# The front of a two-block kernel: modulation chunks in turns of shift and scale, tokens pair by pair, x by tiles

## The reference, cut to what matters

```python
mod = silu(cond) @ w_mod + b_mod            # for x and for ctx: shift, scale, gate of 1024 each, and more for the next layer
y = x * rsqrt(mean(x * x, -1) + 1e-6) * norm_pre
h = y * (1 + scale) + shift                 # the tokens; the same for ctx with its own modulation
px, pc = h_x @ w_in_even, h_ctx @ w_in_even # then rope, differential attention, short convolution, gates, ...
lam = ...exp of two dot products of lam_a   # used in the attention, together with subln
```

## Time and profile before

| | us |
|---|---|
| median of 3 runs | 1631.51 (1627.53 to 1632.32) |
| span of the profiled execution | 1629.8 |
| TensorE matmuls busy | 1520.9 (93%) |
| TensorE weight loads | 1289.6 (79%) |
| VectorE / ScalarE / GpSimd busy | 743.1 / 670.7 / 407.3 |

### The profile page before, as it was taken

How to read it: one execution, slowest core, us unless ns; L and a number is a source line. 1 busy time by engine, 2 the same in 40 slices (tenths; PEclk the granted TensorE clock), 3 DMA queues, 4 the chain that set the end, 5 groups by cost and what they waited for, 6 DMA issues and landing times. The chain is left out here.

```text
span 1629.8 us, 29981 instructions
## 1 busy us (share of the span) xinstructions
PE 1520.9 (93%) x12637; PEld 1289.6 (79%) x12637; DVE 743.1 (46%) x1258; ACT 670.7 (41%) x1098; POOL 407.3 (25%) x106
## 2 busy tenths in 40 slices
PE   4999998889989999998999999978879999999998
PEld 4888897777778888987879897847868888888786
DVE  5344247678645511137854424468654333433002
ACT  5301326666653311137754544372354344344212
POOL 1322221211030243230012432200043343444342
PEclk9999999999999999999999999999999999999999
DMA  9344463335040032046220431000021323222321
GB/s 375 114 156 156 157 180 73 83 80 130 1 174 33 3 130 96 31 147 162 47 104 28 153 123 68 1 0 4 4 105 52 109 98 103 103 82 73 129 90 65
DMA packets 32600, 155.78 MB, mean 96 GB/s; under 512 B 6745, under 2 KB 8281, under 8 KB 18017
## 3 DMA queue, kind: packets, MB, share of 16 engines
q1 hardware_dynamic: 31456, 153.83, 28.4%
q10 hardware_dynamic: 1024, 0.21, 0.1%
HBM read 132.01 MB, written 2.10 MB: 82 GB/s over the span
## 5 line engine op out<-in xcount | busy, mean ns | idle before, releaser
L215 PE MATMUL banks<-ffn_token_parts,ffu_weight_parts 128*128 128x512 f32 (+1 forms) x1056 | 229.6, 380 | 1.2 <-POOL ffu_weight_parts L196 0.9
L215 PEld LDWEIGHTS banks<-ffn_token_parts,ffu_weight_parts 128*128 128x128 f32 x1056 | 191.7, 188 | 38.9 <-POOL ffu_weight_parts L196 1.1
L196 POOL TENSOR_TENSOR even_weight_parts<-weight_chunk,even_weight_parts 128x2048 fp32r<-128x2048 f32 x15 | 70.2, 4683 | 308.7 <-ACT even_weight_parts L190 308.7
L196 POOL TENSOR_TENSOR ffu_weight_parts<-weight_chunk,ffu_weight_parts 128x2048 fp32r<-128x2048 f32 x22 | 101.6, 4619 | 157.3 <-ACT ffu_weight_parts L190 157.3
L215 PE MATMUL banks<-even_token_parts,even_weight_parts 128*128 128x512 f32 (+1 forms) x672 | 124.8, 345 | 0.0
L993 PE MATMUL banks<-even_token_parts,even_weight_parts 128*128 128x512 f32 (+1 forms) x576 | 122.4, 348 | 0.0
L3235 PE MATMUL banks<-ffd_weight_parts,ffn_f_parts 128*128 128x512 f32 x528 | 120.1, 389 | 1.7 <-PEq L3136 1.7
L215 PEld LDWEIGHTS banks<-even_token_parts,even_weight_parts 128*128 128x128 f32 x672 | 103.6, 188 | 19.4 <-issue 3.8
L3235 PEld LDWEIGHTS banks<-ffd_weight_parts,ffn_f_parts 128*128 128x128 f32 x528 | 99.0, 188 | 22.6 <-issue 2.1
L215 PE MATMUL banks<-sec_token_parts,sec_weight_parts 128*128 128x512 f32 (+1 forms) x528 | 115.0, 375 | 0.3 <-PEq L285 0.3
L3213 DVE SCALAR_TENSOR_TENSOR ffn_conv<-banks,b_ffn_taps,ffn_conv 128x511 f32<-128x511 f32 (+1 forms) x88 | 61.8, 744 | 110.7 <-ACT ffn_conv L3185 107.6
(11 more groups left out here) (468 smaller groups left out, 2796.9 us busy)
## 6 DMA issues: line engine op xcount, KB each, us to landing
weight_chunk<-in_ffn_up SPq DMA_DIRECT2D x22, 1024.0 KB, 4.8
weight_chunk<-in_w_in_even SPq DMA_DIRECT2D x16, 1024.0 KB, 7.1
front_late<-in_w_mod SPq DMA_DIRECT2D x16, 1024.0 KB, 5.0
weight_chunk<-in_w_in SPq DMA_DIRECT2D x13, 1024.0 KB, 5.0
weight_chunk<-in_w_out SPq DMA_DIRECT2D x12, 1024.0 KB, 5.4
weight_chunk<-in_w_in_odd SPq DMA_DIRECT2D x12, 1024.0 KB, 4.8
weight_chunk<-in_ffn_down SPq DMA_DIRECT2D x11, 1024.0 KB, 4.9
front_w<-in_w_mod SPq DMA_DIRECT2D x8, 1024.0 KB, 23.5
```

What stands on the lines that cost most here:

```text
L196: (on or self.nc.gpsimd).tensor_tensor(parts[:, 1], self.env.raw[s][:], parts[:, 0].bitcast(F32), ALU.subtract).then_inc(self.lo_done, 1)
L215: m = self.nc.tensor.matmul(o, w, env.tok[:, tp, k, a:b], start=n == 0, stop=n == 3 * KD - 1)
```

## The change

The eight chunks of the front are taken in turns of shift and scale, so that a pair (one shift, one gain chunk) covers two k tiles. The slots in memory are reordered to match. TensorE interleaves: products of pair q with the chunks of pair q + 1, whose columns follow the low products. The transposes run x first (all eight k), then ctx, and both evacuating engines share both kinds. x is loaded as four tiles, each with its semaphore, and x and ctx have a root each. The value tile is cleared by GpSimd and not by VectorE. Five of the seven small loads move from ScalarE's queue to SP's, behind the bulk; the lambda work, which needs them, moves behind the early tiles. The silu of cond is done before the bias loads are issued.

```diff
+MOD_ORDER = 0, 4, 1, 5, 2, 6, 3, 7
...
-        slot_homes = [env.tok_at + s * slot_bytes for s in range(4)] + [env.parts_at + (2 + s) * slot_bytes for s in range(2)]
-        slot_homes += [homes["head_hi"], homes["pT"] + 8 * NT * D]
+        slot_homes = [env.tok_at + s * slot_bytes for s in (0, 3, 1, 4, 2, 5)] + [homes["head_hi"], homes["pT"] + 8 * NT * D]
...
-        SMALL = 16 * 7
+        SMALL, LATER = 16 * 2, 16 * 5
...
+        turns = [*range(0, 2 * KD, 2), *range(1, 2 * KD, 2)]
...
-                sp.dma_start(env.X[:], A["x"].rearrange("(t p) d -> p t d", p=P)).then_inc(x_in, 16)
+                for t in range(TX):
+                    sp.dma_start(env.X[:, t, :], A["x"][t * P : (t + 1) * P]).then_inc(x_in[t], 16)
                 sp.dma_start(env.CX[:], A["ctx"].rearrange("(t p) d -> p t d", p=P)).then_inc(c_in, 16)
-                for n in range(MOD_FIRST):
-                    if n == 3:
+                for a, n in enumerate(MOD_ORDER):
+                    if a == 1:
                         weights(0)
-                    sp.dma_start(slots[n][:], A["w_mod"][n]).then_inc(w_in[n], 16)
+                    sp.dma_start(slots[a][:], A["w_mod"][n]).then_inc(w_in[a], 16)
                 weights(1)
                 sp.dma_start(tables[:], A["rope"]).then_inc(tables_in, 16)
                 sp.dma_start(exchange[:], A["rope_swap"]).then_inc(tables_in, 16)
-                sp.wait_ge(scaled, TX)
+                sp.dma_start(taps[:], A["conv_b"]).then_inc(later_in, 16)
+                sp.dma_start(env.pre2[:], A["pre_mix"]).then_inc(later_in, 16)
+                sp.dma_start(env.pre_ffn[:], A["pre_ffn"]).then_inc(later_in, 16)
+                sp.dma_start(lam[:], A["lam_a"].partition_broadcast(P)).then_inc(later_in, 16)
+                sp.dma_start(env.subln[:], A["subln"]).then_inc(later_in, 16)
+                sp.wait_ge(scaled, 2)
+                sp.wait_ge(scaled_late, 2)
...
+                nc.gpsimd.memset(v_flat, 0.0).then_inc(cleared, 1)
...
                 pe.wait_ge(cond_ready, 1)
-                pe.wait_ge(small_in, SMALL)
                 mod(0)
+                for i in range(KD // 2):
+                    turn_in(i)
                 mod(1)
                 columns(0)
-                mod(2)
+                for i in range(KD // 2, KD):
+                    turn_in(i)
                 columns(1)
...
+                for i in range(KD, 2 * KD):
+                    turn_in(i)
                 pe.wait_ge(raw_even, KD)
                 pe.wait_ge(raw_odd, KD)
...
+                for q in range(KD // 2):
+                    following = range(2 * q + 2, min(2 * q + 4, MOD_FIRST))
+                    for i, k in enumerate((2 * q, 2 * q + 1)):
+                        token_hi(k)
+                        for n in following[i : i + 1]:
+                            mod(n)
+                    if q < KD // 2 - 1:
+                        for i, k in enumerate((2 * q, 2 * q + 1)):
+                            for f in range(2):
+                                token_lo(k, f)
+                            for n in following[i : i + 1]:
+                                columns(n)
+                    else:
+                        for f in range(2):
+                            for k in (2 * q, 2 * q + 1):
+                                token_lo(k, f)
                 late_mod(0)
                 exchanged(0)
...
+                act.wait_ge(cond_in, 16)
+                nc.scalar.activation(cond[:], cond[:], ACT.Silu).then_inc(cond_ready, 1)
                 act.wait_ge(cleared, 1)
                 for j in range(4):
                     act.dma_start(bmod[32 * j : 32 * j + 2], A["b_mod"][j]).then_inc(bias_in, 16)
...
+                act.wait_ge(mean_c, 1)
+                nc.scalar.activation(ss[:, TX:NT], ss[:, TX:NT], ACT.Sqrt).then_inc(root_c, 1)
+                raw(0)
+                act.wait_ge(inverse_c, 1)
...
+                for i in range(2, KD, 2):
+                    raw(i)
                 ring.hi(act, 0, 0)
...
+                for i in range(KD, 2 * KD, 2):
+                    raw(i)
                 act.wait_ge(raw_odd, KD)
                 for q in range(KD // 2):
-                    act.wait_ge(affine, MOD_FIRST // 2 + 1 + q)
+                    act.wait_ge(affine, 2 * q + 2)
                     for j in range(4 * q, 4 * q + 4):
                         affined(j, job_part(j, 0)).then_inc(hi_done, 1)
                     affined(4 * q + 3, job_norm(4 * q + 3)).then_inc(normed_c_odd, 1)
...
                 for q in range(KD // 2):
-                    dve.wait_ge(affine, MOD_FIRST // 2 + 1 + q)
+                    following = range(2 * q + 2, min(2 * q + 4, MOD_FIRST))
+                    dve.wait_ge(affine, 2 * q + 2)
                     normed(4 * q, normed_x)
                     normed(4 * q + 1, normed_c_even)
                     normed(4 * q + 2, normed_x)
-                    if q < 3:
-                        mod_sum(5 + q)
-                    lo(4 * q)
-                    lo(4 * q + 2)
-                    if q < 3:
-                        affine_part(5 + q)
+                    for i, j in enumerate((4 * q, 4 * q + 2)):
+                        lo(j)
+                        for n in following[i : i + 1]:
+                            mod_sum(n)
+                    for n in following:
+                        affine_part(n)
```

More of the change, by code:

```diff
@@ L729, in _, with turn_in @@
             def _(pe):
[L730 to L733, removed]
+                def turn_in(i):
+                    (x, n, t0, _r), k = jobs[turns[i]]
+                    if i >= 4:
+                        pe.wait_ge(raw_odd if i % 2 else raw_even, (i - 4) // 2 + 1)
+                    if k == 0:
+                        pe.wait_ge(small_in, SMALL)
+                        pe.wait_ge(scaled if t0 == 0 else scaled_c, 2)
+                        if t0 == 0:
+                            pe.wait_ge(scaled_late, 2)
                     for t in range(n):
-                        if k == 0:
-                            pe.wait_ge(*((scaled, t + 1) if t0 == 0 else (scaled_c, t + 1)))
-                        m = nc.tensor.transpose(bank(env, 4 + j % 4, P, t * P), xs[:, t0 + t, k * P : (k + 1) * P], env.ident[:])
+                        m = nc.tensor.transpose(bank(env, 4 + i % 4, P, t * P), xs[:, t0 + t, k * P : (k + 1) * P], env.ident[:])
                     m.then_inc(turned_in, 1)
@@ L1259, in _ @@
+                st.inc(squared(1))
+                st.link(squared(3))
+                dve.wait_ge(squares, 2)
+                nc.vector.tensor_scalar(ss[:, 0:TX], ss[:, 0:TX], 1.0 / D, EPS, ALU.mult, ALU.add).then_inc(mean_ready, 1)
                 dve.wait_ge(root_ready, 1)
-                nc.vector.reciprocal(ss[:], ss[:]).then_inc(inverse_ready, 1)
+                nc.vector.reciprocal(ss[:, 0:TX], ss[:, 0:TX]).then_inc(inverse_ready, 1)
                 dve.wait_ge(inverse_ready, 1)
-                for x, t, at in each[:TX]:
-                    nc.vector.tensor_scalar(xs[:, at, :], x[:, t, :], ss[:, at : at + 1], None, ALU.mult).then_inc(scaled, 1)
+                for t in range(2):
+                    nc.vector.tensor_scalar(xs[:, t, :], env.X[:, t, :], ss[:, t : t + 1], None, ALU.mult).then_inc(scaled, 1)
@@ L1392, in _ @@
                         late_sum(n - 1)
+                    if n == FT:
+                        dve.wait_ge(later_in, LATER)
+                        for j in range(2):
+                            nc.vector.tensor_tensor_reduce(
+                                lam_t[:], lam[:, 2 * j, :], lam[:, 2 * j + 1, :], 1.0, 0.0, ALU.mult, ALU.add, lam_s[:, j : j + 1]
+                            ).then_inc(lam_dot, 1)
+                            dve.wait_ge(lam_dot, j + 1)
+                        st.link(nc.vector.tensor_scalar(env.subln[:], env.subln[:], 1.0 - LAM_INIT0, None, ALU.mult))
                     if 2 <= n < 2 * FT + 2:
```

148 lines of the change are left out of this document (49 added, 99 removed).

## The result

The changed kernel takes 1639.77 us (median of 9 runs, 1634.86 to 1643.36) against 1632.32 us (9 runs) for the kernel before: ratio 1.0045, 95% interval 1.0029 to 1.0061, so 7.5 us slower. The profiled execution took 1643.2 us, its span is 1641.4.

What follows compares the result with a forecast made beforehand. TensorE, busy 93% of the span, was taken as the bound, so front delays pass to the end. First late chunk at 62.0 instead of 58.73 us adds 3.3, giving span 1633.1, plus 1.7 for the median: 1634.8 us; range 1630.0 to 1641.0.

Steps and rivals of the forecast that it cites:

- the case that I held likeliest: Whole kernel: the forecast itself, 1632.5 to 1636.4 us, with one clock dip ahead of the first products; chance 0.50.
- rival 1: Rounds of the front: the clock dips there too, one to three times at 1.7 us each, 1636.5 to 1639.9 us; chance 0.30.
- Start: TensorE's front: chunk 0 runs at 15.6 us, the 16 transposes end by about 20.3, then TensorE waits for W.
- W: Landing of w_mod 4, the first gain's chunk, for which TensorE waits: 22.1 less 1.2 for the small loads, 20.9 us.
- The first products: Ahead of the rounds: GpSimd's weight subtraction, behind ScalarE's copy, ends at W + 9.9; products effectively start at W + 9.2.
- The chain behind the columns: End of each round: columns, gain, affine, hi runs uncovered, a hole of 1.68 us, three more times than before.
- The work of a round: TensorE's hi, chunk, lo and columns of a pair: 6.8 us, 8.5 with the hole; three rounds 25.5 us.
- The dips: Clock in the front: one dip to half speed at the long hole ahead of the first products, 2.1 us as before.
- The sum: First late chunk: W 20.9 + 9.2 + 25.5 + 4.3 = 59.9, with the clock's 2.1, 62.0 us against 58.73.
- An end that stays put: Front's end: bulk gains the full 2.9 us and the first dip is missed or hidden; 1630 to 1633 us; chance 0.12.
- Faster: Front: work always ready from 15.6 us on, without waits for W or between rounds; 1626.5 us; chance 0.05.
- x in pieces slowing the queue: Load queue: x as four tiles adds three starts of 3.0 us on the path to W; 1643.8 us; chance 0.03.

Runs made afterwards that it cites:

- equal pieces side by side: Changed kernel with each round's pieces in blocks (hi, hi, chunk, chunk, lo, lo, columns, columns) instead of in turns: 1638.99 us, ratio 1.0049 to the kernel before.
- the hold above: Kernel before with small loads behind the bulk, SP also holding the second weight chunk and all behind it until the seventh chunk is multiplied: 1629.51 us, ratio 0.9979.
- the first experiment: Changed kernel with 12 unread identity transposes on TensorE in each of the three holes behind a pair's columns: 1637.71 us, ratio 1.0029 to the kernel before.

## Why the prediction was right, and where it was off

1639.77 us lies in the range of 1630 to 1641, on the side of "slower by more than 0.3%", to which I gave 0.36; the interval of the ratio, from 1.0029, just reaches down to 0.3%. It isn't the case that I held likeliest: it is rival 1, dips in the rounds. That it still lies in the range is in part luck, since rival 1 with the two dips that came on top of the one I counted is 1638.2, and what lies above it comes from rounds priced too low, which no rival had.

*Start: right in time, not in what ended it.* First chunk 15.95 (15.6 predicted); second 21.25 (W = 20.9). The sign that I named, a wait for a w_mod load until about 21, didn't come: w_mod 4 landed at 20.8, and TensorE was still at its 16 transposes. They took 3.43 us from start to start, where I had about 2.9 (17.4 to 20.3), and the second sixteen 1.90. The granted clock reads 1.00 in the windows from 17 to 20 us, as it does beside a first chunk of 1.94 us against 1.10 later, so those rows don't explain the slow pace of the start. For the 1.2 us that I credited to the small loads, the run with them put back shows 0.7 at both landings, the kernel before without them 1.6 and 2.2 at w_mod 2.

*The first products: right.* ScalarE's copy at 24.54 holds GpSimd's subtraction to 26.52 to 31.05 (W + 9.9 is 30.8), and the second half of the first k waits for it, to 31.11. Half of it was done by then, as reckoned: an effective start of 30.3 against 30.1. The clearing of the value tile on GpSimd took 2.66 us, inside the bound of 6.8, from 0.74 us on, and costs nothing.

*The chain behind the columns: right.* Three holes of 1.60 us, ended by the affines; 1.68 was predicted, from one row of before.

*The work of a round: mis-sized by 0.65 us.* I took 6.84 us of work and 1.68 of hole, from rows where two k of a kind stand together. In turns the eight hi products of one k take 1.61 (55.93 to 57.54), not 1.46, and the lo products 0.89 (58.57 to 59.46), not 0.71. Twice 0.15 and twice 0.18 are 0.66. Three rounds: 2.0 us. The run with equal pieces side by side comes out at my 8.5. The same error sits in the 2.1 that I took for the dip of the kernel before: that stretch, 22.3 us from the first products to the first late chunk, took 20.8 in the run of that order without dip and stop (the hold above), not the 20.1 of my prices, so the dip was 1.5 of it.

*The dips: the step that failed.* I counted one, of 2.1 us, as in before, and held the rounds' holes to be like the one at 479.27 that left the clock at 1.00. Three stretches came. From 31.11 to 66.82 are 35.71 us; the rest of the first round (9.15 less half a hi, 8.35), two rounds (18.3) and the last pair (4.37) are 31.0; the other 4.7 are the dips, 1.6 each. The row to go by was the dip from 37 on, behind waits of 1.00 and 0.64 us, in the same mix of chunks and products. In five kernels with this chain bare (the kernel after and four experiments; in each the hole ahead of the first products and three in the rounds) 16 of 20 such holes, of 1.6 to 2.2 us, were followed by a dip (4 of 5 and 12 of 15); of the three filled ones none. Why the other four weren't, no run shows.

*The sum.* 62.0 was predicted for the first late chunk, 66.82 measured: 0.3 for the start (with rounding), 2.0 for the rounds, 2.6 for the dips. The time is 5.0 us above the forecast of 1634.8, the front 4.8. That the front's loss is passed on to the end held.

*The other rivals.* An end that stays put didn't come: what starts sooner waits for a gain. Faster: the mechanism was sound (start sooner, keep TensorE in work) but the change throws it away. The small loads alone, with the order of before, are 3.8 and 3.4 us faster than before in two runs. x in pieces slowing the queue: false. With one load w_mod 4 landed at 20.5 instead of 20.8, not 6 us sooner. The Trainium skill (DMA: Bandwidth & Descriptors, section Bandwidth) advises batching to 1 MiB or more; for these loads, queued one behind the other, the pieces of 512 KB cost at most those 0.3 us.

So the change is two things. The small loads bring about 3.5 us. The turns of shift and scale with products as soon as a pair is there cost the rest: from the kernel with the small loads alone to the kernel after the front grows by 11.05 us (55.77 to 66.82), of which idle time of TensorE is 4.3 (holes of 8.2 us against waits and stops of 3.9) and dips 4.7; the other 2 I didn't separate (pieces in turns, transposes at low pace). The best version that ran is the kernel before with the small loads behind the bulk: 1628.1 us.

## What to carry over

Where a value is made by a chain over three engines, place the next independent work between its first and last link, and look at what is multiplied last in a round before you split the work into rounds: 1.6 us of chain became 3.2 us with the clock. Price an instruction from rows in which it has the neighbours that it will have, not from a block of its kind. Put a load that nobody needs yet behind the bulk, and above all take it out of the first wait.

## What was new about the hardware

A bare hole of 1.6 us ahead of products mostly costs as much again: the clock fell to 1.2 GHz behind 16 of 20, and each such stretch lost 1.4 to 1.7 us. The length of the hole alone doesn't decide it: stops of 1.15 and 2.65 us left the clock at 1.00, one of 1.46 us was followed by a dip in one kernel and not in the other, and one of 1.78 us by a dip of double length. Filling the holes with work of no use (the first experiment) brought the front to its end 2.2 us sooner than leaving them bare.

TensorE stops on its own, for 0.2 to 2.65 us, in the middle of a chunk of 64 matmuls, with "issue" as the only cause in the trace. One such stop, with a packet on the instruction queue in it, shrank from 2.65 to 0.71 us when the bulk beside it was held. The other stops point the same way: ahead of each of the 15 such stops in the fronts of nine kernels one packet of 16 KB moved on the instruction queue 2.3 to 2.7 us before TensorE went on, and between 20 and 56 us only six such packets move (counted in four of the kernels). And the stops stand at the same place of the program when they come: behind matmul 33 of 64 in one chunk of the kernel before (0.76 us), of the small loads alone (0.34, and none in the second run) and of that kernel with the hold (0.49). That TensorE waits there for its instructions is still a reading, since no row names them, but it is the one that fits; that the bulk delays their packet rests on one pair of executions.

VectorE was held while GpSimd subtracted: three scalings took 3.87 us (28.24 to 32.1) beside the subtraction that ended at 31.05, and 1.32 at 39.70. The Trainium skill (SBUF — State Buffer, section Who interferes with whom) says that VectorE, where it uses its second port pair, as a scaling can, shares it with GpSimd, and that the one that comes first holds it for its whole instruction; the rows agree. It cost nothing here, since ScalarE's affines released the products.
